# Routing of a mixture-of-experts step: low halves through ScalarE and GpSimd, later slots selected on GpSimd, first gather and up products ahead of TensorE's branch

## The reference, cut to what matters

```python
def hier_moe(xn, w_rg, b_rg, w_re, b_re, w_gate, w_up, w_down):
    x = xn.reshape(B * T, D)                                   # 320 tokens x 1024
    g_logits = (x @ w_rg) + b_rg                               # 4 groups
    g_prob = jax.nn.softmax(g_logits, axis=-1)
    g_sel = jnp.argmax(g_logits, axis=-1)
    e_logits = ((x @ w_re) + b_re).reshape(-1, 4, 8)[g_sel]    # 8 experts of the group
    top_v, top_i = lax.top_k(softmax(e_logits), 2)
    gate = one_hot(g_sel) * g_w * e_w                          # two experts per token
    for g in range(4):
        h = silu(x @ w_gate[g]) * (x @ w_up[g])                # 1024 -> 256, 8 experts
        y = y + (h * gate[:, g]) @ w_down[g]                   # 256 -> 1024
    return y
```

## Time and profile before

| | |
|---|---|
| median of 3 runs | 1282.65 us (1280.17 to 1283.98) |
| profiled execution, its own time | 1280.11 us |
| its span in the trace | 1278.8 us |
| mean granted TensorE clock | 0.985 of full speed |
| PE busy | 1193.4 us, 93% |
| DVE busy | 582.7 us, 46% |
| ACT busy | 400.2 us, 31% |
| POOL busy | 146.0 us, 11% |
| DMA | 340.52 MB, mean 266 GB/s |

### The profile page before, as it was taken

How to read it: one execution, slowest core, us unless ns; L and a number is a source line. 1 busy time by engine, 2 the same in 40 slices (tenths; PEclk the granted TensorE clock), 3 DMA queues, 4 the chain that set the end, 5 groups by cost and what they waited for, 6 DMA issues and landing times.

```text
span 1278.8 us, 20881 instructions
## 1 busy us (share of the span) xinstructions
PE 1193.4 (93%) x8548; PEld 742.7 (58%) x8548; DVE 582.7 (46%) x1163; ACT 400.2 (31%) x739; POOL 146.0 (11%) x184
## 2 busy tenths in 40 slices
PE   6999999999999799999999998989999799999996
PEld 5866679877776433333336776866777544333332
DVE  3764368775545622211235667537454541212113
ACT  3533323263443111111124325455444211111113
POOL 5220022111001011000001130001000101100100
PEclk9999999899999899999999999999999999999999
DMA  9575354368659389999974467703785848999994
GB/s 302 160 225 154 101 173 139 115 221 312 229 189 401 134 323 421 420 421 421 421 295 123 147 239 271 249 17 99 296 298 200 332 186 343 417 422 420 421 418 177
DMA packets 114028, 340.52 MB, mean 266 GB/s; under 512 B 7598, under 2 KB 75514, under 8 KB 86272
## 3 DMA queue, kind: packets, MB, share of 16 engines
q1 hardware_dynamic: 108752, 323.51, 67.4%
q0 software_dynamic: 4736, 14.42, 3.6%
q10 hardware_dynamic: 432, 1.11, 0.3%
HBM read 328.48 MB, written 10.54 MB: 265 GB/s over the span
## 4 chain that ended last, share of the span: by engine, by line
PE 74%; DMA 11%; DVE 7%; ACT 4%; issue 2%; POOL 1%; SPq 1%; DVEq 0%; POOLq 0%; ACTq 0%
PE ps L2369 14%; DMA arena<-in_w_exp_up 11%; PE ps L614 9%; PE ps L615 9%; PE ps L616 9%; PE ps L2444 5%; PE ps L2413 3%; PE ps L1530 3%; PE ps L1544 2%; PE ps L1569 2%; DVE wl L608 2%; PE ps L1615 2%; PE ps L1633 2%; PE ps L2347 1%; PE ps L854 1%
## 5 line engine op out<-in xcount | busy, mean ns | idle before, releaser
L2369 PE MATMUL ps<-arena,mkv 128*64 128x512 f32 x1024 | 226.2, 594 | 14.7 <-DMA arena<-in_w_exp_up 13.9
L614 PE MATMUL ps<-bx,wh 128*128 128x320 f16 (+2 forms) x688 | 192.3, 287 | 11.4 <-DVE bx L2120 4.2
L615 PE MATMUL ps<-bx,wh 128*128 128x320 f16 (+2 forms) x688 | 192.5, 287 | 0.0
L616 PE MATMUL ps<-bx,wl 128*128 128x320 f16 (+2 forms) x688 | 192.3, 287 | 0.0
L608 DVE SCALAR_TENSOR_TENSOR wl<-stg,wh 128x1024 f16<-128x1024 f32 x122 | 153.3, 1296 | 51.4 <-ACT wh L600 51.4
L2369 PEld LDWEIGHTS ps<-arena,mkv 128*64 128x64 f32 x1024 | 77.4, 137 | 158.5 <-issue 157.3
L600 ACT ACTIVATE wh<-stg 128x1024 f16<-128x1024 f32 x122 | 122.4, 1050 | 147.2 <-PE ps L616 129.0
L2584 DVE TENSOR_TENSOR arena<-ps,arena 128x512 f16<-128x512 f32 x64 | 44.1, 689 | 151.1 <-ACT arena L2530 118.0
L2588 DVE COPY arena<-ps 128x1 f32<-128x1 f32 x32 | 5.1, 158 | 192.0 <-PE ps L2391 192.0
L614 PEld LDWEIGHTS ps<-bx,wh 128*128 128x128 f16 x688 | 68.8, 101 | 35.6 <-issue 14.7
L614 PE MATMUL ps<-arena,wh 128*128 128x320 f16 x288 | 86.6, 301 | 0.9 <-ACT mkv L1212 0.9
(11 more groups left out here) (438 smaller groups left out, 1782.9 us busy)
## 6 DMA issues: line engine op xcount, KB each, us to landing
arena<-in_w_exp_gate SPq DMA_DIRECT2D x60, 1024.0 KB, 12.9
arena<-in_w_exp_up SPq DMA_DIRECT2D x60, 1024.0 KB, 15.6
arena<-in_w_exp_down SPq DMA_DIRECT2D x32, 1024.0 KB, 15.5
stg<-in_w_exp_down SPq DMA_DIRECT2D x32, 1024.0 KB, 17.0
arena<-in_cache_mem_k SPq DMA_DIRECT2D x16, 1024.0 KB, 7.7
arena<-in_cache_mem_v SPq DMA_DIRECT2D x16, 1024.0 KB, 5.3
stg<-in_w_in_a SPq DMA_DIRECT2D x28, 512.0 KB, 4.7
stg<-in_w_qkv_c SPq DMA_DIRECT2D x20, 512.0 KB, 4.1
```

What stands on the lines that cost most here:

```text
L614: nc.tensor.matmul(out, wh[:, s, at:at + 128], hi, start=start, stop=False, **flags)
L615: nc.tensor.matmul(out, wh[:, s, at:at + 128], lo, start=False, stop=False, **flags)
L616: return nc.tensor.matmul(out, wl[:, s, at:at + 128], hi, start=False, stop=stop, **flags)
L2369: last = nc.tensor.matmul(ps[64 * j:64 * j + 64, UB, :], xe[:, q % 2, j, k, :], gu[:, g % 2, j, :, k, :], start=(k == 0), stop=(k == KD - ...
```

## The change

1. `moe_open_pe` is new: it holds the first gather and `up(0)`. TensorE runs it before its branch; inside the branch these two are gone.
2. ScalarE copies four of the six transposed pieces as they are, in single precision, to `xraw`, which takes the place of `xn` (so each copy waits until all six pieces are transposed). GpSimd subtracts the high halves from them (`route_pool`). VectorE keeps the low halves of the last two pieces (64 rows each; `xt_last`).
3. The selection matrix for slots 256 to 703 is built by GpSimd in nine chained operations (compare, compare, add for each tile of tokens) where VectorE took six; `rest_ready` tells of it. GpSimd's branch comes after it.
4. Some semaphores are merged: `gate_lo` into `pk_ready`, `tab_in` into `small_in`, `row_pad` into `padded`.

```diff
@@ route_act
+    xraw = xn[:].rearrange("p k t -> p (k t)")[:, 0:2048].rearrange("p (g k c) -> p g k c", g=4, k=KD)
+    pk2 = yh[:, 0:NSLOT - S1]
             nc.scalar.mul(dst, src, rtok[:, 1, g // 2:g // 2 + 1]).then_inc(S["xt_hi"], 1)
+            if g < 4:
+                act.wait_ge(S["xt_ps"], 6 * l + 6)
+                nc.scalar.mul(xraw[:, g], src, rtok[:, 1, g // 2:g // 2 + 1]).then_inc(S["xt_raw"], 1)
@@ route_dve
-        for g in range(6):
-            rows, low = (slice(64, 128), xnh) if g >= 4 else (slice(0, 128), xnl)
-            dst, src = nat_part(g, low)
+        rows = slice(64, 128)
+        for g in (4, 5):
+            dst, src = nat_part(g, xnh)
             dve.wait_ge(S["xt_hi"], 6 * l + g + 1)
-            V.scalar_tensor_tensor(dst[rows], src[rows], rtok[rows, 1, g // 2:g // 2 + 1], nat_part(g, xnh)[0][rows],
-                                   ALU.mult, ALU.subtract).then_inc(S["xt_lo"], 1)
+            V.scalar_tensor_tensor(dst[rows], src[rows], rtok[rows, 1, 2:3], dst[rows], ALU.mult, ALU.subtract
+                                   ).then_inc(S["xt_last"], 1)
...
-        slots(slice(S1, NSLOT))
+    def route_pool(pool, link, l):
+        for g in range(4):
+            pool.wait_ge(S["xt_raw"], 4 * l + g + 1)
+            if g == 0:
+                pool.wait_ge(S["cleared"], 3 * l + 3)
+            else:
+                pool.wait_ge(S["xt_lo"], 4 * l + g)
+            nc.gpsimd.tensor_tensor(nat_part(g, xnl)[0], xraw[:, g], nat_part(g, xnh)[0], ALU.subtract
+                                    ).then_inc(S["xt_lo"], 1)
+        pool.wait_ge(S["xt_lo"], 4 * l + 4)
+        pool.wait_ge(S["pk_ready"], 3 * l + 2)
+        c = slice(S1, NSLOT)
+        for i in range(3):
+            p1, p2 = (rt[:, 13, i, at:at + 1] for at in (5, 6))
+            link(nc.gpsimd.tensor_scalar(pk[:, i, c], iota[:, c], p1, None, ALU.is_equal))
+            link(nc.gpsimd.tensor_scalar(pk2, iota[:, c], p2, None, ALU.is_equal))
+            last = nc.gpsimd.tensor_tensor(pk[:, i, c], pk[:, i, c], pk2, ALU.add)
+            if i < 2:
+                link(last)
+        last.then_inc(S["rest_ready"], 1)
+        pool.wait_ge(S["rest_ready"], l + 1)
@@ moe_open_pe, new: the body of gather_first, then
+        pe.wait_ge(gu_in[g % 2], 64 * (g // 2 + 1))
+        for k in range(KD):
+            if k % 4 == 0:
+                pe.wait_ge(S["xg_act"], 11 * l + k // 4 + 1)
+            for j in range(2):
+                last = nc.tensor.matmul(ps[64 * j:64 * j + 64, UB, :], xe[:, 0, j, k, :], gu[:, g % 2, j, :, k, :],
+                                        start=(k == 0), stop=(k == KD - 1), skip_group_check=True)
+        last.then_inc(M["up_ps"], 1)
@@ moe_pe
-        gather_first()
-        up(0)
         gather_gates()
@@ moe_dve, hidden(q)
+            if q == 0:
+                dve.wait_ge(S["rest_ready"], l + 1)
@@ gather_rest
-            pe.wait_ge(S["pk_ready"], 3 * l + 3)
+            pe.wait_ge(S["rest_ready"], l + 1)
@@ the lists of the engines, each layer
         route_pe(pe, l)
+        moe_open_pe(pe, l)
         moe(pe, l, moe_pe)
...
         clear_pool(pool, 0)
+        route_pool(pool, link, 0)
         moe(pool, 0, moe_pool)
```

More of the change, by code:

```diff
@@ L919, in mlstm_pool @@
         nc.gpsimd.memset(dmat[rows, :, 384:448], 0.0)
-        nc.gpsimd.memset(wlast[rows, :, 0:8], 0.0).then_inc(S["row_pad"], 1)
+        nc.gpsimd.memset(wlast[rows, :, 0:8], 0.0).then_inc(S["padded"], 1)
         pool.wait_ge(S["rows_ready"], 1)
@@ L941, in mlstm_pool @@
         pool.wait_ge(S["decay_ready"], 1)
-        nc.gpsimd.memset(vw[rows], 0.0).then_inc(S["row_pad"], 1)
-        pool.wait_ge(S["row_pad"], 2)
+        nc.gpsimd.memset(vw[rows], 0.0).then_inc(S["padded"], 1)
+        pool.wait_ge(S["padded"], 2)
         pool.wait_ge(S["ml_ev"], 1)
@@ L2257, in route_dve @@
             link(V.reduce_sum(rt[:, 13, :, at:at + 1], pm, AX.X))
[L2259 to L2266, removed]
+        c = slice(0, S1)
+        for i in range(3):
+            p1, p2 = (rt[:, 13, i, at:at + 1] for at in (5, 6))
+            link(V.tensor_scalar(pk[:, i, c], iota[:, c], p1, None, ALU.is_equal))
+            last = V.scalar_tensor_tensor(pk[:, i, c], iota[:, c], p2, pk[:, i, c], ALU.is_equal, ALU.add)
+        last.then_inc(S["pk_ready"], 1)
         dve.wait_ge(S["gexp_ready"], l + 1)
@@ L2280, in route_dve @@
         V.tensor_tensor(xnh[64:128, 2, KD, 0:NE], gate[64:128, 2], xnh[64:128, 2, KD, 0:NE], ALU.subtract
-                        ).then_inc(S["gate_lo"], 1)
+                        ).then_inc(S["pk_ready"], 1)
         for r in range(1, ROUNDS):
             V.tensor_scalar(roff[0:1, NE * r:NE * r + NE], off[0:1, :], float(CAP * r), float(2 * T), ALU.add, ALU.min)
-        slots(slice(S1, NSLOT))
+    def route_pool(pool, link, l):
[10 more added lines that the diff above has]
+        c = slice(S1, NSLOT)
+        for i in range(3):
+            p1, p2 = (rt[:, 13, i, at:at + 1] for at in (5, 6))
+            link(nc.gpsimd.tensor_scalar(pk[:, i, c], iota[:, c], p1, None, ALU.is_equal))
[5 more added lines that the diff above has]
+        pool.wait_ge(S["rest_ready"], l + 1)
     def offset(eng, e):
@@ L2289, in build, with moe_open_pe, part @@
     PARTS = ((xnh, 0), (xnl, 0), (xnh, 1), (xnl, 1), (xnh, 2))
+    def moe_open_pe(pe, l):
+        M, g = ML[l], NPAIR * l
+        pe.wait_ge(S["cleared"], 3 * l + 3)
+        pe.wait_ge(S["pk_ready"], 3 * l + 1)
+        pe.wait_ge(S["xt_hi"], 6 * l + 6)
+        def part(x, i, k, start, stop):
+            return nc.tensor.matmul(ps[:, FIRST[k // 4], 128 * (k % 4):128 * (k % 4) + 128], x[:, i, k, :], pk0[:, i, :],
+                                    start=start, stop=stop, skip_group_check=True)
+        for k in range(KD):
+            if k == 4:
+                pe.wait_ge(S["xt_lo"], 4 * l + 1)
+            for i in range(2):
+                part(xnh, i, k, i == 0 and k % 4 == 0, False)
+        for i in range(2):
+            pe.wait_ge(S["xt_lo"], 4 * l + 2 * i + 2)
+            for k in range(KD):
+                part(xnl, i, k, False, False)
+        pe.wait_ge(S["xt_last"], 2 * l + 2)
+        for k in range(KD):
+            last = part(xnh, 2, k, False, True)
+            if k % 4 == 3:
+                last.then_inc(S["xg_ps"], 1)
+        pe.wait_ge(gu_in[g % 2], 64 * (g // 2 + 1))
+        for k in range(KD):
+            if k % 4 == 0:
[4 more added lines that the diff above has]
+        last.then_inc(M["up_ps"], 1)
     def moe_pe(pe, l, rounds):
@@ L2292, in moe_pe @@
         last_step = NPAIR * rounds - 1
[L2293 to L2305, removed]
-                    part(xnh, i, k, i == 0 and k % 4 == 0, False)
-            for i in range(2):
-                pe.wait_ge(S["xt_lo"], 6 * l + 2 * i + 2)
-                for k in range(KD):
-                    part(xnl, i, k, False, False)
-            pe.wait_ge(S["xt_lo"], 6 * l + 6)
-            for k in range(KD):
-                last = part(xnh, 2, k, False, True)
-                if k % 4 == 3:
-                    last.then_inc(S["xg_ps"], 1)
         def gather_gates():
-            pe.wait_ge(S["gate_lo"], l + 1)
+            pe.wait_ge(S["pk_ready"], 3 * l + 3)
             for i, (t0, n) in enumerate(TILES):
@@ L2622, in moe_pool @@
         M = ML[l]
-        pool.wait_ge(S["pk_ready"], 3 * l + (2 if rounds == 1 else 3))
         for q in range(1, NPAIR * rounds):
```

32 lines of the change are left out of this document (15 added, 17 removed).

## The result

The changed kernel takes **1296.45 us** (median of 4 runs, 1296.12 to 1297.56) against 1281.63 us for the kernel before on the same chip (4 runs, 1280.17 to 1283.98). The ratio is 1.0123 with a 95% interval of 1.0104 to 1.0142: slower by 13 to 18 us. The forecast was 1287.0, with a range to 1293.0. The sign came out right, the size was less than a third of what was measured (+4.4 us against about +15). The right sign is luck: the two terms that made the forecast slower, the held routing (+1.8) and the branch behind `up(0)` (+2.6), measured -2.5 and 0, and the loss came from a term that stood at nothing.

A forecast was written before the change was run, and what follows sets the result against it. TensorE sets the time, except where it waits for expert weights. Later gathers (0.6 + 1.2) and exposed branch (1.6 + 1.0) sum to +4.4 us on 1282.65: 1287.0 us, range 1279.0 to 1293.0.

The forecast's parts named there:

- the held routing: Routing ahead of the first gather: `pk0` comes later, so the gather starts 0.6 us later in layer 0, 1.2 in layer 1.
- the branch behind `up(0)`: TensorE's branch, now between `up(0)` and the gates: 1.6 us stay exposed in layer 0, 1.0 in layer 1, together +2.6.
- a term that stood at nothing: GpSimd's nine slot operations, then flag and branch, ahead of its copies: taken as hidden, at no cost.
- what bounds the stretch before: Around the routing, only TensorE's branch delays the gather; each layer has room of about 4 us.
- the holding of VectorE: Routing chain up to L2222: GpSimd's subtractions hold four two-operand VectorE operations, so it ends at 420.4 instead of 415.87.
- The subtractions: GpSimd's four low-half subtractions during routing: 1.27 us each, ending at 420.1.
- 3.6 us of lead: TensorE's sequencer runs 3.6 us ahead of the array, read at `gather_rest`, hiding that much of the branch under `up(0)`.
- GpSimd's nine: Later slots' selection on GpSimd: 7.7 us in all, from 428.8 to 436.5, then flag and branch, 1 us; hidden.
- the 443.5 that I had as the limit: Time in layer 0 at which GpSimd's copies are wanted; 6 us of slack were claimed for them.
- Rival 4: GpSimd late: compares at 2 us each end the branch at 446, +2.5 us a layer, 1292; chance 0.07.

The follow-up runs named there:

- e5: Changed kernel with the two versions of the expert stage in the other order, the taken one right behind each engine's branch: 1285.47 us, ratio 1.0026.
- e7: Kernel before with gather and `up(0)` ahead of TensorE's branch and later slots on GpSimd behind its branch, low halves on VectorE: 1282.33 us, ratio 1.0001.
- e3: Kernel before with only the first gather and `up(0)` moved ahead of TensorE's branch: 1281.13 us, ratio 1.0015.
- e1: Changed kernel with the later slots' selection back on VectorE in six operations, behind the gates: 1279.73 us, ratio 0.9999.
- e2: Changed kernel with GpSimd's branch ahead of its nine operations instead of behind them: 1279.21 us, ratio 1.0002.
- e8: Changed kernel without two of GpSimd's six compares, so its outputs differ: 1289.96 us, ratio 1.0056.
- e9: Changed kernel with GpSimd's branch ahead of its nine operations in layer 1 only; layer 0 as in the changed kernel: 1289.10 us, ratio 1.0065.
- e10: Changed kernel with GpSimd's branch ahead of its nine operations in layer 0 only; layer 1 as in the changed kernel: 1285.78 us, ratio 1.0048.
- e11: Changed kernel with the taken version right behind the branch on TensorE and GpSimd only; ScalarE and VectorE keep the old order: 1282.61 us, ratio 1.0011.
- e4: Kernel before with only ScalarE's raw copies and GpSimd's four subtractions; TensorE's branch stays ahead of the gather: 1284.77 us, ratio 1.0048.

## Why the prediction was wrong, point by point

- **Right: what bounds the stretch before, and that the branch on TensorE is what stood ahead of the gather.** In the trace after, the "issue" of 3.97 and 3.37 us is gone, and the gather starts behind `pk0`.
- **Right in kind, too large in size: the holding of VectorE.** "If each is held by one subtraction ... the chain gets to L2222 when the last subtraction ends." The rows show three operations held, for 0.6 to 1.0 us each, and others that pass because they begin in the 0.14 us between two subtractions (these end at 416.80, 418.09 and 419.39):

```profile
416.03 0.81 DVE L2209 TENSOR_TENSOR arena<-arena 128x24 f32<-128x24 f32 x1
416.87 0.18 DVE L2228 TENSOR_TENSOR arena<-arena 128x24 f32<-128x24 f32 x1
417.09 1.12 DVE L2229 TENSOR_TENSOR arena<-arena 128x96 bf16<-128x96 f32 x1
...
418.28 1.22 DVE L2234 TENSOR_TENSOR mkv<-arena 128x96 f32<-128x96 f32 x1
```

  A short operation is held to the end of the subtraction beside it, but one operation for each subtraction, and the subtractions reach past the end of the chain: up to L2222 it lost 1.5 us instead of 4.5 (418.21 against 415.87 + 0.88), up to `pk0` 2.3 (421.55 against 418.36 + 0.88), and the gather came 1.6 us sooner instead of 0.6 later. In layer 1, with the 9.83 us taken off, it starts at 1030.06 against 1021.18, 0.95 sooner instead of 1.2 later. The term of +1.8 us measured -2.5. The subtractions, 1.15 us each, were priced well (1.27).
- **Wrong by 2.6 us: the branch behind `up(0)`.** It is hidden, in layer 0 only just: the flag's load stands at 428.8, 4.5 us ahead of the end of `up(0)` at 433.28, and the branch takes 3.5 us and ends at 433.18 (3.3 us in layer 1). I had taken 3.6 us of lead from another place and the longer branch.
- **The step that failed: "GpSimd's nine ... then flag and branch, 1 us ... Hidden."** Each tile costs 1.40 + 1.40 + 1.03 instead of 0.7 + 0.7 + 1.13, so the nine took 12.3 us instead of 7.7, from 427.7 instead of 428.8. That alone costs little: TensorE waited 0.6 us for the ninth of them, and 0.76 and 0.46 us for the copies behind them in e5, where the pause is gone. The flag and the branch took 6.3 us instead of 1, since the row of GpSimd's branch, 52 ns, leaves out the pause behind it, which lay in idle time before the change. Together they ended at 446.3 instead of the 443.5 that I had as the limit, and the limit itself had moved forward with TensorE's gain. TensorE then paused 5.70 us and took 2.0 more for `up(1)` at the low clock in layer 0, 4.91 and 1.6 in layer 1. So a term put at nothing measured 7.8 and 6.6 us. Rival 4 named the place and had a chance of 0.07; its price, 2 us for each compare, was not what made it true, and the 1.40 measured lies below the 1.7 from which it was said to decide. No rival had the pause behind GpSimd's branch.
- **The sum.** Measured in the trace: layer 0 -2.0 + 7.8 = +5.8 us, layer 1 -0.3 + 6.6 = +6.3, 12.1 in all; the span grew by 16.3. Of the rest, 0.9 lies ahead of layer 0's routing and 3.0 in layer 1's memory attention, where the clock fell (below). Both are also there in the trace of e7, which is not slower by its times.

Why no version is faster than the kernel before is only in part settled: e3 and e7 show that a gather that starts in the same pause runs on at the low clock into `up(0)`, and gives 0.9 to 1.5 us back there (8.20 and 8.80 us against 7.33). For e1 and e2 (spans of 1279.0 and 1277.0 us against 1278.8) the measurement can't tell a gain of 1 to 3 us from none, and their clock and the later pairs differ by as much from trace to trace.

## What to carry to other kernels

- A branch's price is not its row. Look at the first row of the branch's target, and ask on each engine whether the pause behind the branch lies in idle time; an operation put ahead of the branch moves the pause onto the path with it. Put the branch as early as its flag allows, and work for an idle engine behind it.
- When an idle engine takes over work, write down the time at which its old work is wanted, with the winnings of the other engines already taken off it.
- A pause of TensorE is paid twice when the clock falls behind it: behind e8's pause of 1.95 us the clock stood at 1.00, behind the changed kernel's of 5.70 and 4.91 us at 0.50 and 0.51.

## What the hardware showed that I had not expected

- A branch to code that does not stand next in line costs 5.0 to 5.6 us behind GpSimd's row in the changed kernel, e8, e9 and layer 1 of e10, 5.3 us on VectorE (e3), and 3.3 to 4.1 us in TensorE's own row, against 0.05 us (GpSimd) and 0.07 us (TensorE) when it does (e5). Between 440.5 and 447 us of the changed kernel, around GpSimd's pause, the table of DMA queues has a row for two packets of instructions:

```profile
q14 instruction: 2, 0.02, 0.7%
```

  The Trainium skill, "Runtime: NRT & Kernel Launch", section "Instruction fetch mechanics", says that a taken branch out of the prefetched window waits for the fetch of its page; e5 agrees. The length is not fixed on GpSimd. In e2 its branch stands at 419.6 us, and the first row of the target already at 422.4, 2.8 us behind it:

```profile
L2680 POOLq COMPARE_BRANCH  x2: 53/54/54, 419.6 to 1018.8; - x2
L2299 POOLq MODIFY_POOL_CONFIG  x2: 8/10/11, 422.4 to 422.5; - x2
```

  In layer 0 of e7 and e10 it is 2.9 and 2.7 us. The DMA share in these three pauses is 0.05 to 0.06, in those of 5.0 to 5.6 us it is 0.75 to 1.03, which would fit a fetch that queues behind the weights' transfers. But the target's code differs too, and TensorE's jump at 665 us in e5 takes 3.35 us at a share of 1.00, no more than its branches in quiet stretches. What sets the length is not shown.
- GpSimd's tensor-scalar form with one input (1.33 to 1.40 us) is dearer than its sum of two tiles (1.03) at the same 448 columns.
- In layer 1's memory attention, around 855 to 876 us, the traces come in three kinds. The granted clock stays at 1.00 in the kernel before, e1 and e10. It falls to 0.50 once, for about 3 us, in e2, e3 and e11, which lose 0.8 to 0.9 us there against the kernel before. It falls twice, for about 6.5 and 3 us, in the changed kernel, e4, e5, e7, e8 and e9, which lose 3.0 to 3.1 us. The row of e2 shows the short fall within a window of 6 us:

```profile
862.00:868.00 6.00, 5.87 (x33) 3.41 (x31) 4.28 (x6) 2.71 (x4) 0.00 (x0) 0.72 0.00 1
```

  What decides it stays open. A difference of up to 3 us between two of these traces can be this, and not the edit.
